# The router of a two-layer trunk: unnormalised turned rows, plain fp32 column tiles and one choice for all tokens

## The reference

```python
h = rms_norm(x, norm_ffn_g[1])            # x * rsqrt(mean(x^2) + eps) * g
logits = h @ w_router                     # 256 x 8
top_logit, top_idx = top_k(logits, 2)
gates = softmax(top_logit)
# each expert e takes the rows of h that chose it:
y[tok] += gate * ((silu(h[tok] @ w_gate[e]) * (h[tok] @ w_up[e])) @ w_down[e])
x = x + y;  out = rms_norm(x, norm_final_g)
```

## Time and profile before

| | us |
|---|---|
| median of 3 runs | 1543.22 (1540.04 to 1543.8) |
| profiled execution, its own time | 1542.4 |
| its span, first to last instruction | 1540.6 |
| TensorE busy (matmul) | 1464.1 |
| VectorE busy | 413.6 |
| ScalarE busy | 328.4 |
| GpSimd busy | 28.6 |

### The profile page before, as it was taken

The page is one execution under the profiler, slowest core; times in us unless marked ns, Lnnn a source line. Parts: engine busy times, 40 slices in busy tenths (PEclk is TensorE's granted clock), DMA queues, the critical chain, the costliest instruction groups (busy, mean ns, idle before and its releaser), DMA issues.

```text
span 1540.6 us, 34120 instructions
## 1 busy us (share of the span) xinstructions
PE 1464.1 (95%) x15645; PEld 897.5 (58%) x15645; DVE 413.6 (27%) x640; ACT 328.4 (21%) x477; POOL 28.6 (2%) x43
## 2 busy tenths in 40 slices
PE   4999899999999976999999999999999999999993
PEld 3986899999799964345345345345344354354352
DVE  3454554444565764110110100100100100000101
ACT  4332544334548732100000000000000000000001
POOL 1000000000001101000000000000000000000000
PEclk9998999999999998999999999999999999999997
DMA  9530455555454317899999999999999999999950
GB/s 301 176 110 28 151 192 185 176 186 191 137 157 135 134 55 299 293 391 420 363 398 414 376 393 405 379 396 399 385 396 391 392 402 389 388 405 382 383 206 30
DMA packets 132570, 438.53 MB, mean 285 GB/s; under 512 B 10602, under 2 KB 63936, under 8 KB 116032
## 3 DMA queue, kind: packets, MB, share of 16 engines
q1 hardware_dynamic: 131232, 432.73, 74.6%
q0 software_dynamic: 1184, 3.50, 0.8%
HBM read 435.15 MB, written 1.05 MB: 283 GB/s over the span
## 4 chain that ended last, share of the span: by engine, by line
PE 92%; DVE 3%; ACT 2%; issue 2%; DMA 1%; SPq 1%; POOL 0%; DVEq 0%; ACTq 0%
PE bank L1161 38%; PE bank L1182 19%; PE bank L790 9%; PE bank L791 9%; PE bank L792 9%; PE bank L1224 2%; ACT high L618 1%; PE bank L1206 1%; PE bank L890 1%; DMA raw<-in_ev_w_in 1%; DVE low L623 1%; PE bank L1197 0%; SPq L731 0%; PE bank L909 0%; PE bank L908 0%
## 5 line engine op out<-in xcount | busy, mean ns | idle before, releaser
L1161 PE MATMUL bank<-ring,arena 128*32 128x512 f32 (+1 forms) x6144 | 585.2, 540 | 0.0
L1161 PEld LDWEIGHTS bank<-ring,arena 128*32 128x32 f32 x6144 | 196.4, 110 | 364.5 <-issue 363.3
L1182 PE MATMUL bank<-ring,arena 128*32 128x256 f32 x5376 | 291.5, 379 | 0.0
L1182 PEld LDWEIGHTS bank<-ring,arena 128*32 128x32 f32 x5376 | 174.7, 110 | 117.1 <-issue 3.1
L623 DVE TENSOR_TENSOR low<-raw,high 128x2048 fp32r<-128x2048 f32 x74 | 169.2, 2290 | 174.2 <-ACT high L618 174.2
L790 PE MATMUL bank<-ht_h,high 128*128 128x256 f32 x672 | 193.0, 287 | 3.3 <-DVE vec L1661 3.0
L791 PE MATMUL bank<-ht_l,high 128*128 128x256 f32 x672 | 191.7, 285 | 0.0
L792 PE MATMUL bank<-ht_h,low 128*128 128x256 f32 x672 | 191.6, 285 | 0.0
L618 ACT ACTIVATE high<-raw 128x2048 fp32r<-128x2048 f32 x74 | 141.5, 1913 | 164.3 <-PE bank L792 160.0
L1988 DVE TENSOR_TENSOR expert_rows<-expert_rows,bank 128x512 f32<-128x512 f32 (+1 forms) x48 | 29.7, 620 | 472.6 <-PE bank L1161 253.7
L790 PEld LDWEIGHTS bank<-ht_h,high 128*128 128x128 f32 x672 | 130.5, 194 | 5.1 <-issue 4.6
(11 more groups left out here) (274 smaller groups left out, 1017.2 us busy)
## 6 DMA issues: line engine op xcount, KB each, us to landing
ring<-in_moe_w_down SPq DMA_DIRECT2D x112, 1024.0 KB, 8.0
ring<-in_moe_w_gate SPq DMA_DIRECT2D x64, 1024.0 KB, 9.4
ring<-in_moe_w_up SPq DMA_DIRECT2D x64, 1024.0 KB, 8.8
ring<-in_moe_w_gate SPq DMA_DIRECT2D x64, 768.0 KB, 5.9
ring<-in_moe_w_up SPq DMA_DIRECT2D x64, 768.0 KB, 6.5
raw<-in_ffn_w_gate SPq DMA_DIRECT2D x14, 1024.0 KB, 5.0
raw<-in_ffn_w_up SPq DMA_DIRECT2D x14, 1024.0 KB, 5.0
raw<-in_ffn_w_down SPq DMA_DIRECT2D x14, 1024.0 KB, 4.9
```

The source lines that it names most:

```text
L1161: ins = mm(ps(use)[q * GRP:(q + 1) * GRP, 0:width], rows[:, k, r * GRP:(r + 1) * GRP], weights[:, q, :, :], start=k == 0, stop=k == DK - 1)
L1182: ins = mm(ps(use)[q * GRP:(q + 1) * GRP, 0:DN], m_act_t[:, r, first + c, :], ring[:, at + c * DM + q * DN:at + c * DM + (q + 1) * DN], st ...
```

## The change

- TensorE turns the rows of `x` itself, not the normalised ones, and `xt` holds them in plain fp32. The gain of the norm is multiplied into the router weights once (`scale_router`), and the factor of each token into its logits.
- The logits are made in plain fp32 with four column tiles of 32 (8 used), each for two of the eight feature blocks (`partial_logits`). A second product with the constant selector `C_QSUM` sums the four parts and turns them.
- Comparison and choice run once for both token tiles. Ranks are two products, the counts two more behind them, copied later. The slots keep their offset of one, and the one-hots compare with numbers one higher. Maximum and difference come behind the selection.
- The rows for the gathers are `x` times the factor: high parts by ScalarE, low parts by VectorE; the second tile's low part is written in two halves between the one-hots. GpSimd's subtraction is gone. The gain is multiplied in where the gathered rows are copied.
- `hn` for extra items is written behind their tables. `vec` has 8 columns more, which one more small load on GpSimd's queue fills, and the constants 8 more.

Runs of removed lines that the printed kernel shows are cut.

```diff
...
@@ -318,10 +321,14 @@
         banks.fill(("ml_t", h), h % 2)
-    norm(3)
-    banks.fill("router_rows", 5)
-    banks.fill("router", 4)
+    for t in range(T):
+        for half in range(2):
+            banks.fill(("xt", t, half), 2 * t + half)
+    for t in range(T):
+        banks.fill(("rparts", t), 5 - t, NQ)
+    banks.fill("router", 6)
     banks.fill("rank", 5)
+    banks.fill("counts", 7)
@@ -470,6 +477,7 @@
         assert taken[0] <= ARENA and T * NE * SLOTS <= NG * D_FF // P * GRP
+        xt, xt_parts, w_router = layout(arena, (T, DK, P), (T, P), (DK, GRP))
@@ -861,7 +870,7 @@
             small_projection("fgate", S_F, FOX_H, 0)
-            pe.wait_ge(vec_loaded, 16 * 3)
+            pe.wait_ge(vec_loaded, 16 * 4)
@@ -1133,17 +1142,50 @@
                     output_piece(1, N_WO1, j, (t,))
-            transposes_of_norm(3)
-            small_projection("router", S_R, NE, 3)
-            small_columns("router", NE)
+            def turned_rows(t):
+                for half in range(2):
+                    use = ("xt", t, half)
+                    open_bank(pe, use)
+                    pe.wait_ge(*drained(("wout", 1, 2 * t + half)))
+                    for c in range(4):
+                        k = 4 * half + c
+                        last = nc.tensor.transpose(ps(use)[:, c * P:(c + 1) * P], x[:, t, k * P:(k + 1) * P], ident)
+                    last.then_inc(fill_sem(use), 1)
+            def partial_logits(t):
+                use = ("rparts", t)
+                open_bank(pe, use)
+                for half in range(2):
+                    pe.wait_ge(*drained(("xt", t, half)))
+                    for q in range(NQ):
+                        k = 4 * half + q
+                        ins = mm(ps(use)[q * GRP:(q + 1) * GRP, 0:P], w_router[:, k, :], xt[:, t, k, :],
+                                 start=half == 0, stop=half == 1)
+                        if half:
+                            ins.then_inc(fill_sem(use), 1)
+            for t in range(T):
+                turned_rows(t)
+            pe.wait_ge(router_ready, 1)
+            for t in range(T):
+                partial_logits(t)
+            open_bank(pe, "router")
+            for t in range(T):
+                pe.wait_ge(*drained(("rparts", t)))
+                last = mm(ps("router")[:, t * NE:(t + 1) * NE], xt_parts[:, t, :], cst[:, C_QSUM:C_QSUM + NE],
+                          start=True, stop=True)
+            last.then_inc(fill_sem("router"), 1)
+            open_bank(pe, "rank")
             pe.wait_ge(rsel_ready, 1)
-            open_bank(pe, "rank")
             rk = ps("rank")
-            mm(rk[:, 0:NE], u_inc, r_sel[:, 0, :], start=True, stop=True)
...
+            mm(rk[:, 0:T * NE], u_inc, r_sel.rearrange("p t e -> p (t e)"), start=True, stop=False)
+            mm(rk[:, NE:2 * NE], ones, r_sel[:, 0, :], start=False, stop=True).then_inc(fill_sem("rank"), 1)
+            open_bank(pe, "counts")
+            for t in range(T):
+                last = mm(ps("counts")[:, 0:NE], ones, r_sel[:, t, :], start=t == 0, stop=t == T - 1)
+            last.then_inc(fill_sem("counts"), 1)
@@ -1202,6 +1244,12 @@
                 for t in range(T):
+                    if k == 0:
+                        pe.wait_ge(all_sel_ready, T * half + t + 1)
+                    if (half, k) == (0, 0):
+                        pe.wait_ge(hn_split, t + 1)
+                    if (half, k, t) == (0, DK // 2, 0):
+                        pe.wait_ge(hn_split, 3)
@@ -1267,11 +1315,8 @@
                 pe.wait_ge(over_xg_ready, 2 * (item - NE) + 2)
-            pe.wait_ge(hn_split, 1)
-            pe.wait_ge(all_sel_ready, T)
                 gather(0, k)
-            pe.wait_ge(all_sel_ready, 2 * T)
@@ -1458,11 +1503,39 @@
                 mix_high_part(4 + h, ("ml_t", h), vec[:, V_HEAD + h:V_HEAD + h + 1])
-            squares(3, ("wout", 1))
...
+            def squares_of_router(t, half):
+                act.wait_ge(*drained(("wout", 1, 2 * t + half)))
+                cols = slice(half * 512, half * 512 + 512)
+                fn(hn[:, t, cols], x[:, t, cols], ACT.Square, accum_out=ssq[:, 3, t, half:half + 1]).then_inc(
+                    ssq_ready, 1)
+            def scaled_high(t, cols):
+                fn(hn_h[:, t, cols], x[:, t, cols], ACT.Copy, scale=rstd[:, 3, t:t + 1]).then_inc(hn_high, 1)
+            def rstd_of_router(t):
+                act.wait_ge(inv_ready, T * 3 + t + 1)
+                fn(rstd[:, 3, t:t + 1], inv_ms[:, 3, t:t + 1], ACT.Sqrt, scale=float(DM)).then_inc(rstd_ready, 1)
+                act.wait_ge(rstd_ready, T * 3 + t + 1)
+            fn(unread[:, :], inv_ms[:, 2, :], ACT.Sqrt)
+            for half in range(2):
+                squares_of_router(0, half)
+            rstd_of_router(0)
+            scaled_high(0, slice(0, DM))
+            squares_of_router(1, 0)
+            act.wait_ge(*filled(("xt", 0, 0)))
+            fn(xt[:, 0, 0:4, :].rearrange("p k c -> p (k c)"), ps(("xt", 0, 0)), ACT.Copy).then_inc(
+                drain_sem(("xt", 0, 0)), 1)
+            squares_of_router(1, 1)
+            for t in range(T):
+                act.wait_ge(*filled(("rparts", t)))
+                fn(xt_parts[:, t, :], ps(("rparts", t))[:, 0:P], ACT.Copy).then_inc(drain_sem(("rparts", t)), 1)
+            rstd_of_router(1)
+            for half in range(2):
+                scaled_high(1, slice(half * 512, half * 512 + 512))
+            fn(unread[:, :], inv_ms[:, 3, :], ACT.Exp)
@@ -1471,8 +1544,8 @@
                 fn(xg_all[:, half * FIRST_ITEMS:(half + 1) * FIRST_ITEMS, k, :],
-                   ps(use)[:, 0:GATHERED].rearrange("p (i s) -> p i s", i=FIRST_ITEMS), ACT.Copy).then_inc(
-                       drain_sem(use), 1)
+                   ps(use)[:, 0:GATHERED].rearrange("p (i s) -> p i s", i=FIRST_ITEMS), ACT.Copy,
+                   scale=vec[:, V_GAIN + k:V_GAIN + k + 1]).then_inc(drain_sem(use), 1)
@@ -1528,7 +1601,8 @@
             for row, src in ((V_CONV, w["od_conv_w"][0].rearrange("t (k p) -> (t k) p", p=P)),
-                             (V_POOL, as_rows(w["ev_pool_scale"][0])), (V_HEAD, w["od_head_norm_g"][0])):
+                             (V_POOL, as_rows(w["ev_pool_scale"][0])), (V_HEAD, w["od_head_norm_g"][0]),
+                             (V_GAIN, as_rows(w["norm_ffn_g"][1]))):
@@ -1563,8 +1637,6 @@
             load_gain(4, w["norm_final_g"])
-            pool.wait_ge(hn_high, 1)
-            nc.gpsimd.tensor_tensor(hn_l, hn[:, :, :], hn_h.bitcast(F32), ALU.subtract).then_inc(hn_split, 1)
@@ -1635,6 +1707,14 @@
                 return b[:, None, :].to_broadcast([P, T, n])
+            def scale_router():
+                dve.wait_ge(gate_w_loaded, 48)
+                steps.done(V.memset(w_router, 0.0))
+                V.tensor_tensor(w_router[:, :, 0:NE], w_small[:, :, S_R:S_R + NE],
+                                vec[:, V_GAIN:V_GAIN + DK, None].to_broadcast([P, DK, NE]), ALU.mult).then_inc(
+                                    router_ready, 1)
@@ -1892,61 +1972,100 @@
                 last.then_inc(over_sel_ready, 1)
-            def one_hot_first(half):
+            def one_hot_first(half, t):
                 items = slice(half * FIRST_ITEMS, (half + 1) * FIRST_ITEMS)
-                for t in range(T):
...
+                out = sel_all[:, t, half * GATHERED:(half + 1) * GATHERED]
+                V.tensor_tensor(out.rearrange("p (i s) -> p i s", i=FIRST_ITEMS),
+                                cst[:, None, C_IOTA + 1:C_IOTA + 1 + SLOTS].to_broadcast([P, FIRST_ITEMS, SLOTS]),
+                                r_slot[:, t, items, None].to_broadcast([P, FIRST_ITEMS, SLOTS]),
+                                ALU.is_equal).then_inc(all_sel_ready, 1)
+            def add_output(t, nh):
+                use = ("wout", 1, 2 * t + nh)
+                quarter = x[:, t, nh * 512:(nh + 1) * 512]
+                dve.wait_ge(*filled(use))
+                V.tensor_tensor(quarter, quarter, ps(use), ALU.add).then_inc(drain_sem(use), 1)
+            def turned_part(t, half):
+                use = ("xt", t, half)
+                dve.wait_ge(*filled(use))
+                V.tensor_copy(xt[:, t, 4 * half:4 * half + 4, :].rearrange("p k c -> p (k c)"), ps(use)).then_inc(
+                    drain_sem(use), 1)
+            def scaled_low(t, cols, n):
+                dve.wait_ge(hn_high, n)
+                V.scalar_tensor_tensor(hn_l[:, t, cols], x[:, t, cols], rstd[:, 3, t:t + 1],
+                                       hn_h[:, t, cols].bitcast(F32), ALU.mult, ALU.subtract).then_inc(hn_split, 1)
+            def gathered_rows(k):
+                use = ("gather", 0, k)
+                dve.wait_ge(*filled(use))
+                V.tensor_scalar(xg_all[:, 0:FIRST_ITEMS, k, :],
+                                ps(use)[:, 0:GATHERED].rearrange("p (i s) -> p i s", i=FIRST_ITEMS),
+                                vec[:, V_GAIN + k:V_GAIN + k + 1], None, ALU.mult).then_inc(drain_sem(use), 1)
```

(95 more changed lines are left out.)

20 lines of the change are left out of this document (3 added, 17 removed).

## The result

The changed kernel takes 1522.57 us (median of 4, 1522.38 to 1525.34) beside 1542.9 (4 runs): ratio 0.9879, interval [0.9856, 0.9902], 18.7 us by the ratio. In a second measurement it was 1524.21 beside 1541.03: 0.9895 [0.9866, 0.9923]. The direction was right, the size was not, though the part of the kernel that the forecast worked out came out nearly as forecast.

The account below looks back on a forecast made before the run. TensorE carries 92% of the chain, so only the serial 24.9 us router stretch where it stands still could yield. First expert piece 12.2 us earlier, less 0.7 for the clock, gives 11.5: forecast 1531.5 us, range 1527 to 1537.

Parts of the forecast that it names:

- What is cut from this stretch moves the rest left by the same amount.: From the first expert piece on, TensorE runs item after item; 12.2 us earlier there carries through if weights are there.
- The clock ahead of the router: The new order was laid over the old projection end, 577.02; the start's load and router weights were taken as hidden.
- The projection's end to the logits: Router, 577.02 to 581.5: logits stand there instead of at 586.92, as split, 24 matmuls and copy of rows go.
- To the selection: Router, logits to selection at 583.2: 1.7 us for both token tiles at once, where 7.2 us passed before.
- Rank to the first one-hot: Router after selection: two rank products of 0.60 and 0.43, a product and a one-hot; TensorE starts at 585.2.
- To the first piece: Gathers: second tile's gather waits until 586.4, first gather ends at 587.1, first expert piece starts at 589.7, 12.2 us earlier.
- The blocked addition: VectorE's line 1922, 4.56 us: 4.3 us of it taken as blocking by GpSimd's 4.48-us subtraction.
- The clock behind the router: Granted clock low until about 591, so 1.3 us of the first expert piece run at half speed: 0.7 us lost.
- The two rules weighed: Router: transposes not counting as clock activity would cost 0.4 us at the last logits; semaphore increments in partial_logits 0.1 more.
- VectorE's queue behind the start, SyncE's queue and the weights: Item 0 and later: four products of 2.8 us ahead of the first one-hot, and SyncE's loads, cause no TensorE wait.
- The rivals: Clock low longer 0.10, clock never down 0.08, line 1922's own time 0.03, tiles not overlapping 0.03, weights short 0.03, slower 0.02.
- the five cases counted as faster: Likeliest gain 9.5 to 13.5 us 0.71, clock low longer 0.10, clock never down 0.08, line 1922 0.03, tiles 0.03.

Follow-up runs that it names:

- the second pair of traces: Both kernels profiled again, unchanged: the kernel before measured 1.0013 against itself, the changed kernel 0.9895 against the kernel before.
- that with 235 instructions: Changed kernel with 235 semaphore increments more on TensorE's list, in its two waits at the start: 1542.17 us, ratio 1.0004.
- the start's edits alone: Kernel before with only the change's 8 more constants, 8 more vector columns loaded and turned, and shifted buffers: ratio 0.9996.
- The per-tile experiment: Changed kernel with the five comparisons looped over token tiles one after the other again: 1523.24 us, ratio 0.9871.
- the eight matmuls: Changed kernel with eight 128x512 matmuls, result not used, on TensorE ahead of the wait for the selection: 1522.03 us, ratio 0.9874.

## Why the prediction was wrong

- *"What is cut from this stretch moves the rest left by the same amount."* This is the step that failed. It held as far as the last expert item and failed in the wait behind it: the 13.2 us of issue at the end had no term in the sum and no rival; I took them as fixed. Over the traces the wait is 14.1 us on average with the loop's head at its old place (5 profiles of kernels made from the one before) and 7.3 at the changed kernel's place. These 6.8 us come with the change and have nothing to do with what it computes: TensorE's program is 20 instructions longer ahead of the loop, and waits for two packets there in place of five. Together with the router's 12.4 less 0.6 they make 18.6 us. The ratio gives 18.7, but its interval is 15 to 22 us and the second measurement gave 16.2, so the close agreement is chance; in the second pair of traces, for one, the last combination's matmuls took 1.0 us longer in the changed kernel.
- *The clock ahead of the router.* I took the profiled execution's start of the router, 577.0, as that of every run. It is not even that of the same kernel: the end of the projection lies between 572.1 and 577.4 in the profiles above, that with 235 instructions left out. In the first pair of profiles this made 2.8 us. The averages over kernels with the old and the new router, 576.3 and 574.5, differ by 1.9 with a spread of 5; the start's edits alone gave nothing, and whether a part of it belongs to the change is open.
- *The projection's end to the logits*: forecast 4.5 us (577.0 to 581.5), measured 4.42 (574.16 to 578.58).
- *To the selection*: forecast 1.7, measured 1.7 (to 580.29). The per-tile experiment gives 0.8 on VectorE, as forecast.
- *Rank to the first one-hot*: forecast 1.4 from selection to its start, measured 1.04; the products took 0.36 and 0.23 at full clock where I had put 0.60 and 0.43 from the slower rows.
- *To the first piece*: forecast 5.1 from the one-hot's start, measured 5.3. Whole stretch: forecast 12.7, measured 12.5. The row of line 1164 shows the column tiles in parallel: the last eight instructions 0.55 us, forecast 0.53.
- *The blocked addition*: forecast 4.3; in the kernel before the selection came 4.3 earlier without it, and the stretch was 3.7 shorter, as 0.7 of gate products come into the path there.
- *The clock behind the router*: forecast at half until near 591, that is 14.0 behind the projection's end; it rose at about 588.1, 13.9 behind it. The term of 0.7 was 0.76 (3.47 against 2.71 for the first piece). This hit is in part luck. The forecast's ground was a rise as long after the dense gathers' begin as before, 2.9 us and a little, which from 586.4 is 590 and not 591; measured were 5.1 us, from 583.1 to 588.1.
- *The two rules weighed*: the granted clock was 1.00 from 574 to 580, so the last logits did not run at half speed and the 0.4 us did not occur. The step to the logits came 0.1 us shorter than forecast; nothing of the other 0.1 is seen.
- *VectorE's queue behind the start, SyncE's queue and the weights*: TensorE waits for none of them in item 0, and the seven items take the same 875.1 us. The four products took 2.72 us and the first one-hot ended at 617.7; TensorE asked at 622.4.
- The rivals: none occurred. The one that was missing is the place of TensorE's loop in its program. Of the chances, the five cases counted as faster add up to 0.95 and not 0.94, which changes nothing.

## What to carry to other kernels

A wait that the profile ascribes to nothing ("issue") ahead of a loop or a jump is a term of its own: before forecasting a change in the number of instructions ahead of it, ask whether it fetches instructions, and read the queue of instruction fetches in both profiles, inside the wait and not only in total. To credit an edit, split the gain by stretches and hold only the edited one against it; to test the rest, shift the program without changing the work. The prediction of a serial stretch from rows of single instructions was good to 0.2 us in 12.5, with single steps off by up to 0.4 that partly cancelled, so an error of several microseconds was to be sought outside it. The granted clock can take back or double a gain one step later (1.0 us became 0.6, 0.75 became 1.5): read the next dense instructions too before crediting the edit.

## What the runs showed of the hardware

- Ahead of the last combination, in a loop that is skipped five times, TensorE waits 13.2 to 14.7 us while five instruction packets of 16 KB are fetched, or 7.1 to 7.5 us while two are. A shift of the loop by 20 or 21 instructions, and by 36 with the eight matmuls, gives the shorter wait; 235 more on top of the 20 bring the longer one back; moving only the loop's tail by 21 changed nothing. Why the head's place matters, and where the limit lies, is open.
- A semaphore increment on TensorE's list takes about 0.125 us: 118 of them held it for 14.8 us.
- The granted clock in a stretch of thin work differed between executions of one program: 0.66 and 0.89 in 115 to 130 us of the kernel before. 25 runs of that kernel lie between 1534.86 and 1546.81 us.
- The clock's fall behind the router (0.50 in 582 to 584) was avoided by 2.1 us of matmuls with an unused result, in two profiles.
